# A two-layer decoder step: half of a down projection behind each pair of feed-forward steps, weight work moved from GpSimd to VectorE, and the first pair's products in another order

## The reference

```python
x = x + y                                            # y from the mixer
y, fbuf = conv_ffn(rmsnorm(x, p['norm_ffn'][l]), ...)
x = x + y

def conv_ffn(x, buf, w_up, conv_w, conv_b, w_down):
    u = x @ w_up                                     # 1024 -> 2 x 3072
    uc = causal_dwconv(concat(buf, u), conv_w, conv_b)   # width 3
    val, gate = uc[..., :D_FF], uc[..., D_FF:]
    return (jax.nn.gelu(gate) * val) @ w_down, new_buf   # 3072 -> 1024
```

## Time and profile before

| | before |
|---|---|
| median of 3 runs | 2578.41 us (2577.18 to 2578.7) |
| the profiled execution, own time | 2577.07 us |
| its span in the trace | 2575.3 us |
| TensorE busy | 2502.3 us (97%) |
| VectorE busy | 1773.7 us (69%) |
| ScalarE busy | 1054.4 us (41%) |
| GpSimd busy | 1166.8 us (45%) |
| granted TensorE clock, mean | 0.994 |

### The profile page before, as it was taken

One profiled execution on the slowest core, in us unless ns is written; L12 is line 12 of the kernel. 1 busy time (PEld: TensorE's weight loads), 2 busy tenths in 40 slices (PEclk: granted clock), 3 DMA queues, 4 the chain that ended last, 5 costly groups with the idle time before them and its releaser, 6 DMA issues.

```text
span 2575.3 us, 41719 instructions
## 1 busy us (share of the span) xinstructions
PE 2502.3 (97%) x16316; PEld 2423.6 (94%) x16316; DVE 1773.7 (69%) x2620; ACT 1054.4 (41%) x1842; POOL 1166.8 (45%) x727
## 2 busy tenths in 40 slices
PE   8999989999999999999999999998999999999998
PEld 7999989999999999998999999898999999999998
DVE  8877488666666666676656555748866666666668
ACT  5655243333333333334444444624333333333333
POOL 2001265555555555544333333126655555555551
PEclk9999999999999999999999999999999999999999
DMA  4112211111111111134233232411111111111112
GB/s 143 46 44 88 79 33 50 50 50 50 50 50 50 47 41 45 46 130 126 90 97 105 94 98 85 156 50 33 50 50 50 50 50 50 50 47 42 44 47 86
DMA packets 102770, 170.17 MB, mean 66 GB/s; under 512 B 11909, under 2 KB 50309, under 8 KB 102318
## 3 DMA queue, kind: packets, MB, share of 16 engines
q1 hardware_dynamic: 96622, 145.19, 18.0%
q10 hardware_dynamic: 5952, 22.30, 2.3%
HBM read 145.93 MB, written 26.23 MB: 67 GB/s over the span
## 4 chain that ended last, share of the span: by engine, by line
PE 58%; DVE 30%; ACT 5%; issue 4%; POOL 2%; DMA 0%; DVEq 0%; SPq 0%; ACTq 0%
PE psum L1262 12%; PE psum L1044 11%; DVE line L2208 7%; DVE line L2630 5%; PE psum L1166 5%; PE psum L1168 5%; PE psum L1167 5%; PE psum L1323 3%; PE psum L1327 3%; PE psum L1325 3%; DVE x L2564 2%; ACT line L1858 2%; DVE line L2643 2%; PE psum L1357 2%; PE psum L1381 2%
## 5 line engine op out<-in xcount | busy, mean ns | idle before, releaser
L945 POOL TENSOR_TENSOR w_lo<-w_raw,w_hi 128x512 fp32r<-128x512 f32 x280 | 436.7, 1567 | 397.2 <-ACT w_hi L1884 396.5
L1166 PE MATMUL psum<-xn_hi,w_hi 128*128 128x352 f32 x1536 | 501.4, 326 | 26.5 <-DVE xn_lo L2520 15.6
L1168 PE MATMUL psum<-xn_lo,w_hi 128*128 128x352 f32 x1536 | 496.6, 323 | 0.0
L1167 PE MATMUL psum<-xn_hi,w_lo 128*128 128x352 f32 x1536 | 495.7, 323 | 0.0
L1262 PE MATMUL psum<-h_hi,w_hi 128*128 128x352 f32 x1032 | 334.5, 324 | 4.5 <-DVE x L2564 4.5
L1262 PE MATMUL psum<-h_hi,w_lo 128*128 128x352 f32 x1032 | 333.2, 323 | 0.0
L1262 PE MATMUL psum<-h_lo,w_hi 128*128 128x352 f32 x1032 | 332.4, 322 | 0.0
L945 POOL TENSOR_TENSOR w_lo<-w_raw_third,w_hi 128x512 fp32r<-128x512 f32 x148 | 225.9, 1529 | 224.6 <-ACT w_hi L1884 224.6
L1166 PEld LDWEIGHTS psum<-xn_hi,w_hi 128*128 128x128 f32 x1536 | 289.9, 189 | 37.5 <-DVE line L2606 18.3
L2564 DVE TENSOR_TENSOR x<-psum,x 128x1056 f32<-128x1056 f32 x176 | 220.8, 1255 | 101.9 <-PE psum L1262 100.4
L1168 PEld LDWEIGHTS psum<-xn_lo,w_hi 128*128 128x128 f32 x1536 | 290.9, 189 | 0.0
(11 more groups left out here) (355 smaller groups left out, 5583.6 us busy)
## 6 DMA issues: line engine op xcount, KB each, us to landing
w_raw<-in_w SPq DMA_DIRECT2D x194, 256.0 KB, 2.7
w_raw<-in_w SPq DMA_DIRECT2D x56, 512.0 KB, 3.5
w_raw_third<-in_w SPq DMA_DIRECT2D x94, 256.0 KB, 2.7
k_pages<-in_cache_k SPq DMA_DIRECT2D x128, 64.0 KB, 1.9
v_pages<-in_cache_v SPq DMA_DIRECT2D x128, 64.0 KB, 2.0
scratch_line<-scratch_row ACTq DMA_DIRECT2D x1, 4608.0 KB, 21.0
x<-in_x SPq DMA_DIRECT2D x8, 528.0 KB, 8.6
scratch_x<-x ACTq DMA_DIRECT2D x1, 4224.0 KB, 14.2
```

Source lines behind the costliest of these rows:

```text
L945: pool.tensor_tensor(out_lo, op_src(op), out_hi.bitcast(F32), ALU.subtract).then_inc(q["op_lo"], 1)
L1166: pe.matmul(out, op_hi(op)[:, k, :], hi, start=start, stop=False, skip_group_check=True)
L1167: pe.matmul(out, op_lo(op)[:, k, :], hi, start=False, stop=False, skip_group_check=True)
L1168: return pe.matmul(out, op_hi(op)[:, k, :], lo, start=False, stop=True, skip_group_check=True)
```

## The change

It has four parts.

**Half a down projection behind each pair.** `half_down(f)` holds for pairs 2 to 21. Behind pair 2g+2 TensorE makes outputs 0 to 3 of down g, behind pair 2g+3 outputs 4 to 7. Downs 10 and 11 stand whole at the end. Each of these pairs has its own convolution between the four additions of its half. PSUM banks, weight slots, buffers of loaded halves and the order of the weights in memory follow (`up_banks`, `slots`, `raw_halves`). Within a pair the order of the steps stays as it was, but for pair 0.

**Low parts and sums on VectorE.** The low parts of b12, t4 and, from pair 1 on, b11 and b21 are made by VectorE, as are the sums t3 and t4. GpSimd keeps the low parts of t1, t2, b22, t3 and of the down weights.

**The first pair.** Its order becomes k1a, k1b, p1, p2, k2a, k2b, `norm_sum`, p6, p5, p7, p3, p4; the products that need sums of activations come last. The weight sums of pair 0, and the sums and low parts around the last output tile, move in VectorE's queue; the first highs and the copy of p1 move ahead of the root in ScalarE's.

**The whole products** outside the blocks (`unit` without `release`) run over thirds outside and tiles inside; the matmuls are the same.

```diff
-WEIGHTS = ("b11", "b21", "t1", "t2", "b22", "t3", "b12", "t4")
-EARLY = 4
+FIRST_ROUND = ("k1a", "k1b", "p1", "p2", "k2a", "k2b", "p6", "p5", "p7", "p3", "p4")
+EARLY = 2
...
+def half_down(f):
+    return 2 <= f < FT - 2
+
+def half_outs(f):
+    return range(4 * (f % 2), 4 * (f % 2) + 4)
...
+def on_dve(op):
+    return op[0] in ("b12", "t4") or op[0] in ("b11", "b21") and op[1] > 0
...
-                for f in range(2):
+                for f in range(FT):
                     pair(f)
-                for g in range(GROUPS - 1):
-                    for f in (2 * g + 2, 2 * g + 3):
-                        pair(f)
-                    if l == 0 or g < GROUPS - 2:
-                        down(g)
+                    if half_down(f):
+                        down((f - 2) // 2, half_outs(f), f)
                 if l == 0:
-                    down(GROUPS - 1)
+                    down(GROUPS - 2, range(KT), FT - 1)
+                    down(GROUPS - 1, range(KT), FT - 1)
...
             def ffn(l, a_end):
                 for op in OP:
...
-                    low(l, op, op_hi(op), op_lo(op))
-                    if op[0] == "t1":
-                        third_sums(l, op[1])
-                    if op[0] == "t2":
-                        fourth_sums(l, op[1])
+                    if not on_dve(op):
+                        low(l, op, op_hi(op), op_lo(op))
...
+                    conv_start(f, 0)
+                    conv_end(f, 0)
+                    outs(0)
+                    if f < FT - 1:
+                        weight_low(l, ("b11", f + 1))
+                    conv_start(f, 1)
+                    outs(1)
+                    conv_end(f, 1)
+                    if f < FT - 1:
+                        first_sums(l, f + 1)
+                        weight_low(l, ("b21", f + 1))
+                    outs(2)
+                    gated(f)
+                    outs(3)
+                    if f < FT - 1:
+                        fourth_sum(l, f + 1)
+                        low_h(f)
```

More of the change, by code:

```diff
@@ new lines, with lows, slots @@
+RAW_PARTS = ("b11", "b21", "b12", "b22")
+RAW_BUFS = 6
+STEP, OP, HALVES = ffn_order()
+def on_dve(op):
+    return op[0] in ("b12", "t4") or op[0] in ("b11", "b21") and op[1] > 0
+def lows():
+    had, out = dict(op_lo=0, dve_lo=0), {}
+    for op in OP:
+        name = "dve_lo" if on_dve(op) else "op_lo"
+        had[name] += 1
+        out[op] = name, had[name]
+    return out, had
+LOW, LOWS = lows()
+def slots():
+    held, place = [0] * 4, {}
+    for op in OP:
+        q = min(range(4), key=lambda n: (held[n], n))
+        if op[0] == "d" and op[1] >= GROUPS - 2:
+            q = (1, 0, 3, 2)[op[2]]
+        place[op] = q, held[q]
+        end = ("d", op[1], 2 * op[2] + 1) if op[0] == "d" else (done_at(*op), op[1])
+        held[q] = STEP[end] + 1
+    return place, held
@@ new lines, with unit_places, half_over @@
+SLOT, SLOTS_END = slots()
+def unit_places():
+    units = {}
+    for f in range(FT):
+        if f > 3 and f % 2 == 0:
+            units["down", f // 2 - 2, 0], units["down", f // 2 - 2, 1] = len(units), len(units) + 1
+        units["up", f, 0], units["up", f, 1] = len(units), len(units) + 1
+    for g in (GROUPS - 2, GROUPS - 1):
+        units["down", g, 0], units["down", g, 1] = len(units), len(units) + 1
+    return units
+UNIT = unit_places()
+assert len(UNIT) == F_UNITS
+def half_over(half):
+    what, n = half[0], half[1]
+    if what == "d":
+        return [LOW[half]]
+    return {"b11": [LOW["t3", n]], "b21": [LOW["t4", n]], "b12": [LOW["b12", n], ("t3_sum", n + 1)],
+            "b22": [LOW["b22", n], ("t3_sum", n + 1)]}[what]
@@ L191, in raw_halves, with half_rank @@
+def half_rank(half):
+    what, n = half[0], half[1]
+    return OP[half if what == "d" else (dict(b11="t3", b21="t4", b12="b12", b22="t3")[what], n)]
+def raw_halves():
+    held, loads, out = [None] * RAW_BUFS, [0] * RAW_BUFS, {}
+    for half in HALVES:
+        if half[0] == "d" and half[1] >= GROUPS - 2:
+            b = 2 + half[2]
+        else:
+            b = min(range(RAW_BUFS), key=lambda n: (-1 if held[n] is None else half_rank(held[n]), n))
         loads[b] += 1
-        out[half] = b, loads[b], ends[b]
@@ L193, in raw_halves @@
-        ends[b] = over(half)
-    return out, loads, ends
-HALF, HALF_LOADS, HALF_ENDS = raw_halves()
+        out[half] = b, loads[b], held[b]
+        held[b] = half
+    return out, loads, held
+HALF, HALF_LOADS, HALF_LAST = raw_halves()
 def half_place(half):
@@ L1894, in pair @@
+                state(0, 0)
+                copied(l, 0, "p6")
+                copied(l, 0, "p5")
+                top(l, ("t4", 0))
+                state(0, 1)
+                before_next(0)
+                for f in range(1, FT):
+                    late = not half_down(f - 1)
                     if late:
                         tap(f - 1, 1)
-                    elif f:
-                        tap(f - 1, 0)
-                        tap(f - 1, 1)
-                        high("b11", f)
-                        gelu(f - 1)
-                        high("b21", f)
-                        high("t1", f)
-                        high_h(f - 1)
-                        high("t2", f)
@@ L1931, in ffn @@
[L1931 to L1932 removed]
+                    top(l, ("t4", f))
+                    before_next(f)
                 for i in range(4):
[L1934 removed]
+                    top(l, ("d", GROUPS - 2, i))
                 tap(FT - 1, 0)
```

523 lines of the change are left out of this document (289 added, 234 removed).

## The result

The changed kernel takes 2537.19 us (median of 4 runs, 2536.6 to 2538.53), the kernel before took 2577.8 us (4 runs, 2576.96 to 2578.7) on the same chip: a ratio of 0.9843, with a 95% interval of 0.9826 to 0.986. That is 40.6 us less, and 5 us more than the 2532 us forecast. The profiled execution took 2536.6 us (span 2534.7); the forecast's sum for it was 2531.1 us.

A forecast was written before the change was run, and what follows sets the result against it. TensorE, busy 97%, was taken as the bound, losing time in stops on ScalarE and VectorE: 2577.1 - 26.1 - 24.1 + 3.0 left over + 1.2 at block starts = 2531.1 us, median 2532 us, range 2522 to 2556.

The forecast's parts named there:

- The stops vanish: Behind each layer's first pair, TensorE's 38 and 35 stops go, each costing idle time + 0.27 us: 26.1 and 24.1 us.
- Why they vanish: VectorE's convolution at the next pair's head, slowed beside GpSimd (2.01 against 1.33 us), delays gelu, copy and `value_second` behind it.
- the walk: Step-by-step timing of one pair and its half, without TensorE stops; convolution rows 1.33 us, thinnest margin 0.7 us at output 3.
- I let both stops there vanish: Pairs 22 and 23, without a half behind them: convolution over some 6.5 us behind p4, against 9.6 us for p2.
- the first weight of down 10: Its slot frees only behind k2b of pair 23; high and low part within p4's 1.92 us: 0.3 to 1 us stop per layer.
- The blocks' starts: Pair 0 of each layer: p4 newly waits some 7 us behind root and reciprocal; +0.6 us each, bounds -3 and +4.
- The rival of 2524 us: No 7 us wait at the block starts, as VectorE reaches the root earlier or the clock holds: 2 x 4 us less; 12%.
- Unit order at nothing: In the whole products, running thirds outside costs nothing, as the matmuls are the same.
- VectorE some 200 us busier: Sign that the forecast is right: VectorE some 200 us busier in all, GpSimd some 400 us less.
- every half stopping at output 3: Slower rival: VectorE's chain is late for TensorE's fourth output in all 40 halves, costing 64 us: 2596 us; 4%.
- The return of stops by the shared port: Rival: VectorE meeting GpSimd or late additions bring back 40 stops, 15 to 27 us: 2547 to 2559 us; 16%.
- Sum: For the profiled execution: 2577.1 - 26.1 - 24.1 + 3.0 + 1.2 = 2531.1 us; 2532 us as median.

The follow-up runs named there:

- the sums-ahead kernel: The changed kernel with VectorE's first two weight sums of the next pair set ahead of the second addition to x in each half down projection: 2566.57 us.
- the order alone: The changed kernel with all low parts of weights and each pair's third and fourth sums back on GpSimd: 2543.4 us, ratio 0.9871.

## Why the prediction was right, and where it was off

- **The stops vanish** (-26.1 and -24.1 us): right, with its price. Between 411 and 1060 us there is no stop; the round is 65.5 us as forecast; a stop costs idle + 0.26 us (the sums-ahead kernel).
- **Why they vanish**: half right. I put the lateness down to the conv at the head of the next pair with GpSimd beside it, and gave the walk rows of 1.33 us. With GpSimd back beside VectorE and one row of 2.25 us in each half there is still no stop. So the half down projection behind each pair, with the pair's convolution between its additions, is the cause; the moved operations are worth some 6 us, most of it in pairs 0 to 2.
- **"I let both stops there vanish. New is the first weight of down 10 ... a stop of 0.3 to 1 us"**: this is the step that failed. The first weight cost 0.39 us. What I didn't walk was ScalarE's queue: it holds that weight's three sisters ahead of the tap, so output 2 stopped 1.94 us, and in this execution the clock fell behind it. 4.2 us are lost in downs 10 and 11 of layer 0, and setting the taps ahead gave 3.05 us of them back (3.7 us by the times). The rest of layer 0 was 4.7 us longer than its forecast.
- **The blocks' starts** (+0.6 us each): the mechanism was right (a wait of 6.3 and 5.5 us for 7, slow starts behind it), the size was +1.55 and +1.75, inside its bounds. The rival of 2524 us ("no 7 us wait") didn't come, and none of five kernels that shortened this wait brought its gain: others took its place.
- **Unit order at nothing**: not refuted by the times; the trace has up to 1.3 us there.
- **VectorE some 200 us busier**: wrong, 17 us. The moved operations show 170 us. What I left out is that the rest gets shorter when it seldom meets GpSimd: the 192 convolution rows by 91 us together, the 96 copies of two columns by 26.
- **Rivals**: every half stopping at output 3 would take a chain some 1 us longer, and one of 1.45 us more made it so. The return of stops by the shared port didn't happen even where GpSimd was there, with one slowed row in a half.
- **Sum**: 4.7 + 0.9 in layer 0, 0.9 + 1.15 in layer 1, less 2.2 outside the blocks, is 5.5 us, the difference of 2536.6 and 2531.1.

## What to carry to other kernels

Walk the steady part for its margins, but walk the ends too, with every engine's queue: the last rounds have another order, and what was left to lose here lay in ScalarE's queue of one pair. When a long wait can be had back by moving its operand, sum the late starts over the whole stretch before and after: if the sum stays, the queue of the engine behind it is the likely bound; in this case cutting work out of it helped, and reordering it or moving some of it to GpSimd didn't. A cover that is long enough makes it matter little which engine does the small operations under it. And a slow clock behind a short stop is to be looked for in several profiles before it is put down to the stop.

## What the hardware showed that I had not expected

Where both read two operands from SBUF, VectorE and GpSimd don't slow each other, they take turns. In the order alone, VectorE and then GpSimd:

```profile
732.54 1.33 DVE L2343 SCALAR_TENSOR_TENSOR line<-line,columns,line 128x1072 f32<-128x1072 f32 x1
733.90 2.25 DVE L2781 SCALAR_TENSOR_TENSOR line<-line,columns,line 128x1072 f32<-128x1072 f32 x1
...
746.31 1.25 DVE L2712 TENSOR_TENSOR x<-psum,x 128x1056 f32<-128x1056 f32 x1
```

```profile
732.81 2.20 POOL L743 TENSOR_TENSOR w_lo<-w_raw_third,w_hi 128x512 fp32r<-128x512 f32 x1 [0.61 <-ACT w_hi L1800]
...
746.29 1.31 POOL L743 TENSOR_TENSOR w_lo<-w_sum,w_hi 128x512 fp32r<-128x512 f32 x1
```

The low part, issued at 732.81 while the first row runs to 733.87, ends at 735.01, 1.14 us after that row's end, where it takes 1.28 us alone; the second row ends at 736.15, 1.14 us after the low part's end, where it takes 1.33 us alone. So a meeting costs nearly what the other's instruction still has to run: here 1.06 and 1.11 us were left, and each lost 0.92. It is no single case. In the trace of before 125 convolution rows began while a low part or sum of GpSimd ran, and every one ended 1.13 to 1.14 us behind it, whether it showed 1.7 or 2.4 us; 99 of GpSimd's began under such a row and ended 1.14 to 1.16 us behind it. If each only slowed the other, these ends would spread with the overlap. The addition that reads one operand from PSUM ran beside a low part (746.31, 1.25 us) with neither longer; 51 such pairs in before show 1.24 to 1.26 and 1.28 to 1.32 us. The Trainium skill (SBUF — State Buffer, "SBUF: two separate sides") calls the shared port pair an exclusive lock, which a VectorE operation with two SBUF inputs takes against a GpSimd one that reads SBUF; the trace agrees with it in these rows. By that rule, too, a slowed row is no property of the row but of what was issued ahead of it, and a chain should be walked with the overlap that it really has.
